# Gate and up projections of two SwiGLU blocks as seven block products (Strassen) in place of eight, with weight sums on VectorE and normed operands

## What is computed

```python
def rms_norm(x, g):
    xf = x.astype(jnp.float32)
    y = xf * lax.rsqrt(jnp.mean(xf * xf, axis=-1, keepdims=True) + EPS)
    return (y * g.astype(jnp.float32)).astype(x.dtype)

def swiglu(h, w_gate, w_up, w_down):
    return (jax.nn.silu(h @ w_gate) * (h @ w_up)) @ w_down

...
        x = x + 0.5 * swiglu(rms_norm(x, ffn1_norm), ffn1_w_gate, ffn1_w_up, ffn1_w_down)
```

## Time and profile before

| | us |
|---|---|
| median of 3 runs | 3105.68 |
| lowest, highest | 3100.5, 3107.89 |
| the profiled execution | 3104.45 |
| its span, first to last instruction | 3102.7 |

### The profile page before, as it was taken

One profiled execution on the slowest core, in us unless ns is written; L12 is line 12 of the kernel. 1 busy time (PEld: TensorE's weight loads), 2 busy tenths in 40 slices (PEclk: granted clock), 3 DMA queues, 4 the chain that ended last, 5 costly groups with the idle time before them and its releaser, 6 DMA issues.

```text
span 3102.7 us, 34506 instructions
## 1 busy us (share of the span) xinstructions
PE 2801.1 (90%) x13915; PEld 2308.7 (74%) x13915; DVE 1308.4 (42%) x1911; ACT 1180.3 (38%) x1653; POOL 1166.8 (38%) x556
## 2 busy tenths in 40 slices
PE   6999977865797999999999999488989999999997
PEld 5777756755786888887888788267878888878885
DVE  6556546867665322222222421468853222222223
ACT  5444436631454422223322422367744222232222
POOL 2112102131004555456555643300045555565554
PEclk9999988977998999999999999799999999999998
DMA  3223212153115233333323332100023333333332
GB/s 128 95 86 121 89 62 82 68 172 97 35 35 190 89 99 98 97 108 95 102 90 101 100 127 82 72 8 8 1 95 95 95 95 102 101 101 105 106 105 75
DMA packets 96334, 280.10 MB, mean 90 GB/s; under 512 B 26344, under 2 KB 26536, under 8 KB 96048
## 3 DMA queue, kind: packets, MB, share of 16 engines
q1 hardware_dynamic: 96176, 277.91, 27.5%
HBM read 245.30 MB, written 32.57 MB: 90 GB/s over the span
## 4 chain that ended last, share of the span: by engine, by line
PE 75%; DVE 11%; ACT 4%; issue 4%; DMA 2%; POOL 2%; SPq 0%; POOLq 0%; DVEq 0%; ACTq 0%
PE ps L326 22%; PE ps L327 22%; PE ps L328 22%; ACT t L342 3%; DVE t L941 2%; PE ps L817 1%; DVE t L935 1%; PE ps L805 1%; PE ps L467 1%; DVE t L930 1%; DVE t L601 1%; POOL t L1644 1%; DVE t L957 1%; ACT t L343 1%; DVE t L955 0%
## 5 line engine op out<-in xcount | busy, mean ns | idle before, releaser
L326 PE MATMUL ps<-t 128*128 128x512 f32 (+3 forms) x3528 | 1356.0, 384 | 55.5 <-ACT t L342 21.5
L342 ACT ACTIVATE t<-t 128x1024 fp32r<-128x1024 f32 (+6 forms) x1029 | 781.2, 804 | 1583.1 <-PE ps L328 676.5
L327 PE MATMUL ps<-t 128*128 128x512 f32 (+3 forms) x3528 | 1332.8, 378 | 0.0
L328 PE MATMUL ps<-t 128*128 128x512 f32 (+3 forms) x3528 | 1332.8, 378 | 0.0
L391 POOL TENSOR_TENSOR t<-t 128x1024 fp32r<-128x1024 f32 x363 | 875.8, 2416 | 1066.4 <-ACT t L342 1066.4
L326 PEld LDWEIGHTS ps<-t 128*128 128x128 f32 (+1 forms) x3528 | 669.6, 190 | 201.8 <-issue 57.2
L327 PEld LDWEIGHTS ps<-t 128*128 128x128 f32 (+1 forms) x3528 | 670.5, 190 | 122.0 <-issue 5.3
L328 PEld LDWEIGHTS ps<-t 128*128 128x128 f32 (+1 forms) x3528 | 670.0, 190 | 121.8
L342 ACT ACTIVATE t<-ps 128x512 fp32r<-128x512 f32 (+6 forms) x359 | 183.5, 545 | 238.9 <-PE ps L817 122.1
L1860 DVE SCALAR_TENSOR_TENSOR t<-ps,t 128x512 f32<-128x512 f32 x192 | 132.7, 691 | 318.0 <-PE ps L328 277.2
L1916 POOL TENSOR_TENSOR t<-t 128x512 fp32r<-128x512 f32 x84 | 108.8, 1295 | 332.3 <-ACT t L342 332.3
(11 more groups left out here) (145 smaller groups left out, 1724.6 us busy)
## 6 DMA issues: line engine op xcount, KB each, us to landing
t<-in_wts_dram SPq DMA_DIRECT2D x363, 512.0 KB, 3.5
t<-pj SPq DMA_DIRECT2D x42, 512.0 KB, 5.5
pj<-t SPq DMA_DIRECT2D x32, 512.0 KB, 3.3
t<-in_rpb_dram SPq DMA_DIRECT2D x8, 736.0 KB, 8.2
t<-in_xT_dram SPq DMA_DIRECT2D x8, 512.0 KB, 10.3
t<-grow_d SPq DMA_DIRECT2D x8, 512.0 KB, 6.2
t<-beta_d SPq DMA_DIRECT2D x8, 512.0 KB, 6.7
t<-in_xT_dram SPq DMA_DIRECT2D x16, 256.0 KB, 3.9
```

Source lines behind the costliest of these rows:

```text
L326: e.matmul(out, ah, bh, start=start, stop=False)
L327: e.matmul(out, ah, bl, start=False, stop=False)
L328: return e.matmul(out, al, bh, start=False, stop=stop)
L342: return e.activation(out, in_, fn, scale=scale)
```

## The change

The gate tile and the up tile of a pair are taken as a matrix of 2 x 2 blocks (rows: gate, up; columns: the first and second 512 of the 1024 inputs), and the 512 tokens of a half with the 8 rows of X as another (first and second four rows, first and second 256 tokens). The product of the two is made of seven block products by Strassen's method in Winograd's form, each of 4 x 3 matmuls of 256 columns, in place of eight. For this

- DVE makes four sums of weight blocks for each pair (128 x 512 each, `dve_part` with part 0) and the small parts of these sums (128 x 1024, parts 1 and 2); ACT makes their large parts; POOL keeps the small parts of the plain blocks (part 0, 1024 wide, and part 3, 512 wide);
- the split weights lie in a ring of 8 blocks of 128 x 512, all used by one pair, freed product by product;
- the token operands are normed before the matmul (`dve_blocks`): X times gain times factor, then four sums of 256 columns, a large part of 1792 columns (ACT) and a small part of 1792 columns (DVE), for each of four k. For half 0 they are made in the second half of the output projection, for half 1 during the down steps of groups 3 and 4 of half 0;
- the seven products leave PSUM by one ACT copy (P1) and seven additions of 256 columns on DVE;
- for groups 3 to 5 all pairs come first and then the three down steps; the last, narrow pair of each half is made with plain blocks in 60 matmuls of 256 columns in place of 24 of 512.

```diff
+    PRODUCTS = [("P1", 0, 6), ("P6", 3, 1), ("P2", 1, 4), ("P5", 2, 0), ("P3", 5, 5), ("P7", 4, 2), ("P4", 6, 3)]
+    PAIR_PARTS = [(0, 1), (2, 3), (4, 5), (6,)]
...
+                upto = min(FT, sum(GROUPS[:g + 1]) + 1) if g < 3 else FT
...
+    def dve_part(e, w, q):
+        if q >= len(parts) or parts[q][1] in (None, 3):
+            return
+        n, x = parts[q]
+        S = sums_of(n)
+        if x:
+            w.wait_ge(w_hi, (n, x))
+            src, hi, lo = part_places(q)
+            e.tensor_tensor(lo, src, hi.bitcast(F), SUB).then_inc(*w_sum_lo.up((n, x)))
+            return
...
+        e.tensor_tensor(S[:, 0, :], up[:, first], up[:, second], ADD).then_inc(*w_sum.up((n, 0)))
+        e.tensor_tensor(S[:, 2, :], gate[:, first], up[:, first], SUB)
+        w.wait_ge(w_sum, (n, 0))
+        e.tensor_tensor(S[:, 1, :], S[:, 0, :], gate[:, first], SUB).then_inc(*w_sum.up((n, 1)))
+        w.wait_ge(w_sum, (n, 1))
+        e.tensor_tensor(S[:, 3, :], gate[:, second], S[:, 1, :], SUB).then_inc(*w_sum.up((n, 2)))
...
+    def dve_blocks(e, w, P, s, k, ready):
...
+        e.scalar_tensor_tensor(flat2(T[:, 4:6, :]), X[:, k + 4, h], NH(stage, k + 4), B_.rs[:, h], MUL, MUL)
+        e.scalar_tensor_tensor(flat2(T[:, 6:8, :]), X[:, k, h], NH(stage, k), B_.rs[:, h], MUL,
+                               MUL).then_inc(*t_w.up(key("B")))
...
+    blocks_at = {2: [("new", 0)], 3: [("new", 1), ("small", 0)], 4: [("new", 2), ("small", 1)],
+                 5: [("new", 3), ("small", 2)], 6: [("small", 3)]}
...
+    def pe_pair(e, w, P, s, j, n):
+        key = lambda p: (P.name, j, p)
+        lows = {0: (w_lo, n), 1: (w_lo, n), 2: (w_sum_lo, (n, 1)), 3: (w_sum_lo, (n, 1)), 4: (w_sum_lo, (n, 2)),
+                5: (w_sum_lo, (n, 2)), 6: (w_lo, n + 1)}
+        for name, b, t in PRODUCTS:
+            pe_slot(w, key(name), [(f_add, key(READ[name])) if READ[name] else (f_cp, key(name))], banks)
+            w.wait_ge(*lows[b])
+            hi, lo = ring_blocks(B_.WH, n, b, 1), ring_blocks(B_.WL, n, b, 1)
+            for k in range(4):
+                w.wait_ge(b_lo, (P.stage, s, k))
+                m = mm3(e, P.place(j, name), (hi[:, tok[k]], lo[:, tok[k]]), (P.F.TH[:, k, t, :], P.F.TL[:, k, t, :]),
+                        k == 0, k == 3)
+            m.then_inc(*f_prod.up(key(name)))
...
+    def dve_pair(e, w, P, s, i, j, n):
...
+        dve_part(e, w, q + 4)
...
+        add("U2", P.sum(j, "U2"), "P6", "P1")
...
+        add("C11", sg[:, first], "P2", "P1")
+        add("U4", P.sum(j, "U4"), "P5", "U2")
+        add("C12", sg[:, second], "P3", "U4")
+        dve_part(e, w, q + 5)
...
+        add("C22", ab[:, second], "P7", "U4")
+        add("U3", P.sum(j, "U3"), "P7", "U2")
+        dve_part(e, w, q + 6)
+        add("C21", ab[:, first], "P4", "U3")
+        w.wait_ge(f_silu, (P.name, j))
+        w.wait_ge(f_add, key("C21"))
+        e.tensor_tensor(ab, ab, sg, MUL).then_inc(*f_mul.up((P.name, j)))
...
+            if what == "gate_up" and i < FT - 1:
+                j = FT * s + i
+                act_part(e, w, q + 3)
...
+                act(e, P.sum(j, "P1"), P.place(j, "P1"), ACT.Copy).then_inc(*f_cp.up((P.name, j, "P1")))
+                hidden()
...
+                act_part(e, w, q + 4)
+                act_part(e, w, q + 5)
+                w.wait_ge(f_add, (P.name, j, "C12"))
+                act(e, P.gate(j), P.gate(j), ACT.Silu).then_inc(*f_silu.up((P.name, j)))
+                act_part(e, w, q + 6)
...
+                pool_part(e, w, q + 3)
+                small()
+                late.append(FT * s + i)
+                for x in (4, 5, 6):
+                    pool_part(e, w, q + x)
```

More of the change, by code:

```diff
@@ L187, in ffn_stream @@
             n += 4
[L188 to L202, removed]
+        plan = []
+        for s in range(2):
+            i = 0
+            for g in range(len(GROUPS)):
+                upto = min(FT, sum(GROUPS[:g + 1]) + 1) if g < 3 else FT
+                for i in range(i, upto):
+                    if i < FT - 1:
+                        plan.append(("gate_up", s, i, stream_pair(name, FT * s + i, gate[i])))
+                    else:
+                        plan.append(("gate_up", s, i, stream([gate[i]])))
+                i = upto
+                plan.append(("down", s, g, stream([down[g] + m for m in range(4)])))
         return plan
@@ L397, in pe_half, with ring_blocks @@
-    def pe_half(e, w, n, out, half, H, Lo, ready, order=tuple(range(KC))):
+        hi, lo = I_.sp[n % NS]
+        e.tensor_tensor(lo[:], I_.raw[n % NR][:], hi[:].bitcast(F), SUB).then_inc(*w_lo.up(n))
+    flat2 = lambda a: a.rearrange("p a n -> p (a n)")
+    def ring_blocks(W, n, b, count):
+        at = (block_of[n] + b) % 8
+        return flat2(W[:, at:at + count, :])
+    def weights_of(n):
+        if n < N_INPROJ:
+            return I_.sp[n % NS]
+        return ring_blocks(B_.WH, n, 0, 2), ring_blocks(B_.WL, n, 0, 2)
@@ L399, in pe_half @@
+    def pe_half(e, w, n, out, operand, ready, order=tuple(range(KC))):
         hi, lo = weights_of(n)
@@ L404, in pe_half @@
             a = tok[k]
-            m = mm3(e, out, (hi[:, a], lo[:, a]), (H[:, k, halves[half]], Lo[:, k, halves[half]]), i == 0, i == KC - 1)
+            m = mm3(e, out, (hi[:, a], lo[:, a]), operand(k), i == 0, i == KC - 1)
         return m
@@ L455, in pe_inproj @@
                 ready = lambda k: [(p_hi, k), (p_lo, k)]
[L456 removed]
+                m = pe_half(e, w, n, slot(n % 3)[:, halves[0]], rows(0), ready)
             if n == 0:
@@ L1594, in pe_factor, with pe_tile @@
         w.wait_ge(b_acc, (stage, s, KC - 1))
-        e.matmul(p, ONES, B_.acc[:, halves[s]], start=True, stop=True).then_inc(*b_sum.up((stage, s)))
-    def pe_tile(e, w, n, T, s, ready, until, order=tuple(range(KC))):
+        e.matmul(p, ONES, B_.acc[:], start=True, stop=True).then_inc(*b_sum.up((stage, s)))
+    def pe_tile(e, w, n, operand, ready, until, order=tuple(range(KC))):
         p = pe_slot(w, n, until, banks)
-        pe_half(e, w, n, p, s, T.H, T.Lo, ready, order).then_inc(*w_used.up(n))
+        pe_half(e, w, n, p, operand, ready, order).then_inc(*w_used.up(n))
     def act_factor(e, w, stage, s, last):
@@ L1885, in act_ffn, with hidden @@
+                    if s == 1 and P.after == "mixn":
+                        if i == 3:
+                            dve_operand(e, w, 0, o)
+                        if i == final_group:
+                            dve_operand(e, w, 1, o)
+    def act_ffn(e, w, P):
+        late = []
+        def hidden():
+            for j, r in late:
+                w.wait_ge(*P.product(j))
                 if j >= 10:
                     w.wait_ge(w_used, P.end_of[(j - 10) // FT, P.group_of[(j - 10) % FT]])
+                else:
+                    w.wait_ge(w_used, P.out.n(1, KC - 1))
@@ L1919, in pool_ffn @@
                     pool_squares(e, w, P.after, 0, 2 * i + 1)
+            elif what == "gate_up":
+                small()
+                pool_part(e, w, q + 3)
             else:
```

467 lines of the change are left out of this document (306 added, 161 removed).

## The result

The changed kernel takes 3155.92 us (median of 4 runs, 3147.5 to 3159.6) where the kernel before took 3106.61 on the same chip (median of 4, 3100.5 to 3107.89): a ratio of 1.0159, 95% interval 1.0133 to 1.0185. It is slower by 1.6%, inside the range (3080 to 3215), 6 us under the forecast of 3162. The profiled execution is its shortest, 3147.5 us (span 3145.7), 43 us above that of before.

The account below looks back on a forecast made before the run. Both feed-forward stretches were taken as bound by PE's matmuls. From 3104.45 us: -67 + 7 for matmuls, +84 waits in runs, +24 holes, +8 down steps, +2 clock = 3162 us; range of 8 in 10, 3080 to 3215.

Parts of the forecast that it names:

- hole before the first pair: PE's wait before the first pair of a feed-forward part: 12 us, twice, +24 us.
- Part 1: Gate and up matmuls on PE: starts 0.120 us apart, a pair 10.08 us, -67 us; narrow last pairs +7.
- Part 2: Pairs: DVE instructions with two SBUF inputs and POOL's exclude each other; period 12.2 us, PE waits +84 us.
- The schedule by hand: Order of DVE's and POOL's instructions within one pair, DVE never idle: the product ends at 12.1 us, period taken 12.2.
- Part 3: Normed operands: DVE late before the first pair, +24 us; half 1's operands in down steps, 4 us late twice, +8.
- (c): Rival for the pairs: DVE loses every turn, period 13.0, or ACT's Silu comes late; 3210 us and over, chance 0.14.
- The clock: PE's clock may read 0.5 for a few microseconds after each long wait: +2 us; 2 us waits should not lower it.
- (a): Rival for the pairs: POOL and DVE fit together and PE stays the bound; 3058 us, chance 0.12.
- (b): Rival for the pairs: half way, period 10.7 to 11.5 us, waits only in long runs; 3080 to 3125 us, chance 0.18.
- (d): Rival for PE's 256-column matmuls: starts every 0.130 us, no gain; 3115 us with the waits hidden, chance 0.03.

Follow-up runs that it names:

- the first experiment: Changed kernel with POOL's three subtractions per pair replaced by writes of zeros, those small parts left out: 3070.95 us (one run).
- the dose: Changed kernel with POOL's 512 wide subtraction of each pair (part 3) made twice, to the same result: 3242.75 us (one run).
- shorter turns: Changed kernel with POOL's 1024 wide subtraction of part 0 cut into two of 512: 3108.07 us (median of 10), 1.0008 of the kernel before.

## Why the prediction was right, point by point

The two feed-forward parts, from the first matmul of the first pair on, became longer by 20.7 and 23.9 us in the profiled executions; the rest of the program differs by -1.5. So the account is that of the parts:

| term | forecast | measured |
|---|---|---|
| matmuls of the pairs, narrow pairs (measured: by the distance of starts) | -67 + 7 | -60 |
| waits in runs of pairs | +84 | +74.4 |
| hole before the first pair | +24 | +20.9 |
| waits in the down steps of groups 3 and 4, over those of before | +8 | +3.1 |
| slower matmuls (clock and short gaps) | +2 | +17 |
| waits at the parts' ends that before had and after has not | 0 | -10.6 |
| sum | +58 | +44.8 |

- **Part 1** held: starts lie 0.120 us apart in a product (1308.28 to 1309.35 us, nine steps of 0.119). The 109 ns of the Trainium skill (TensorE: Matmul & The Clock Gate, section Back-to-back issue gap) are not reached anywhere in these products.
- **Part 2** held in its mechanism and nearly in size. The schedule by hand had the second sum, POOL, the third sum, POOL's part 0, the fourth sum: it is the order of the rows above. The period is 11.88 and not 12.2, so a wait is 1.71 and not 2.1. Which pairs wait came out as counted in the later runs: the last pair of each run of 4 and the last five of the run of 8 (only four in the last half), for L503 on DVE. In the first run of a half two or three pairs wait, 1.7 to 3.8 us each, where I had three of 2.1; 6.5 us of these waits, in the two second halves, end on POOL's L491, and not on DVE. Together 74.4 for 84. One sign did not come: small parts were to take over 1.3 us, and L503 has a mean of 1.28 and 1.21 to 1.22 in the long run, since POOL stands idle when they start.
- **Part 3** held: each of the two holes is 6.15 + 4.29 us, where I had 12. The waits of the down steps came to 0.63 + 2.0 us in each part where before had 1.09. Two of the sums are a little off and move nothing: four times 5.1 us of operands are 20.4 and not 20.6, and rival (c) adds up to 104 and not 106.
- **The clock** is the term that was mis-sized: +2 in the sum, up to +17 measured. I argued that short waits do not lower it, from a row of attention, and that held in the long runs of the window above (1.00), though not in the last half, where it fell at 3011 us behind waits of 0.51 and 2.42 (0.66 granted from 3010 to 3015). And it fell after the holes and in the first run of a half:

```profile
core 0: us, PE busy (x) PEld busy (x) DVE busy (x) ACT busy (x) POOL busy (x), PEclk, DMA share, GB/s
1045.00:1075.00 30.00, 20.01 (x138) 19.04 (x137) 24.60 (x29) 16.28 (x21) 12.91 (x8) 0.77 0.21 71
...
1460.00:1480.00 20.00, 16.79 (x127) 16.45 (x126) 15.68 (x20) 9.68 (x14) 14.19 (x9) 0.91 0.26 80
```

  Behind the wait that ends at 1051.47 two matmuls of 256 columns start 0.21 us apart (1051.85 and 1052.06), the pace of 1.2 GHz. The 17 us are the growth of all distances between 0.01 and 0.3 us over the nominal one, nearly all of it at 256-column matmuls, behind the holes and in the first runs; they may hold short gaps that are not the clock, and how much these are stays open. It is also a part of why the first experiment was 20 us faster than expected: with the waits went most of the slow matmuls behind them (the growth at 256 columns is 18.4 us in the changed kernel and 4.6 there), the two holes lost 5 us, and the waits in the runs came to 72 us less where I had counted 65.
- **What I did not see**: the kernel before waits some 5 us at the end of each part (2.48 at its last pair), and these waits are gone. That its size nearly cancels the error in the clock is luck.
- The rivals: (a), the two engines fit together, is what the kernel with one gated subtraction on POOL shows, and (b), a period of 10.7 to 11.5, the one with shorter turns (10.77). What keeps the changed kernel from (b) is the one 1024 wide instruction: cut in two, it gives back 1.11 of the 1.80 us over PE's 10.08. (d) is refuted by the distance of the starts, (c) by the period of 11.88 and by the first two sums of the pair shown, 0.68 us each, which are not held up.

The shortest run of the changed kernel is the profiled one, so the medians differ by 49 and the profiles by 43; in the profiles of the experiments the output projection ahead of the first feed-forward part begins 3 to 7 us later than in that of the changed kernel (953.6 to 957.5 in place of 950.8 us; 962.4 in the dose), so that much comes from ahead of the change.

## What to carry to other kernels

Before giving DVE more instructions with two SBUF operands, add up how long POOL reads SBUF beside them, and lay both lists side by side: where two such instructions meet, one of them waits for the whole of the other. A subtraction that POOL makes in 2.4 us and DVE in 1.2 is no help when DVE must stand still for it; give it to DVE, gate POOL's to DVE's PSUM work, or cut it in turns no longer than what DVE can do meanwhile. And a list with no idle time may still hold much waiting, here a fifth of it (198.6 against 161.1 us): look at an instruction's length against its bare length, not at the idle time in front of it.

## What the runs showed of the hardware

- POOL that only writes SBUF does not block DVE at all: with POOL clearing 1008 pieces (128 columns, 0.206 us each) beside them the weight sums took 0.684 to 0.692 us. The Trainium skill (SBUF — State Buffer, section Who interferes with whom) says that such a DVE instruction contends with a GpSimd instruction that reads SBUF, "not with one that only writes it"; the trace agrees.
- The turns alternate. In the rows shown neither engine gets two turns in a row while the other waits: two of POOL's halves with a DVE sum between them, and a POOL instruction reaches into DVE's list at the next boundary. In no row shown here does a DVE instruction wait for two of POOL's. The nearest to it is a product of the dose run at 2969.56 us, which comes 0.05 us before one of POOL's ends and is held by the next as well (2.96 us).
- A blocked DVE instruction ends 0.55 us after the POOL instruction in front of it (1316.89 and 1317.44; 1319.70 and 1320.25), for a bare length of 0.68: some 0.13 us of it lie under the wait.
